# Attention scores as stacked rounded products, and the tile output taken from its bank by ScalarE

## The chip, the cores and the metric

The kernel runs on one core of one Trainium2 chip. Its time is the device time of one launch in microseconds (us); the median of three runs before the change is 2268.42 us (2266.53 to 2269.19).

## What is computed

One step of a one-layer backbone over 1152 tokens: 128 context tokens and 1024 latent tokens, width 1024. A first SwiGLU feed-forward part, an input projection, an attention group beside a recurrent group, an output projection, a second feed-forward part, a final norm. The change is in the attention group, four heads of two score maps each:

```python
q, k = rope(q), rope(k)                      # latent tokens only
k_all = concat(k, cached_k)                  # 1024 + 128 keys of 64 numbers, for each of m = 0, 1
s = einsum('bqhmd,bkhmd->bhmqk', q, k_all) * 64 ** -0.5
p = softmax(s)                               # in float32
pd = p[:, :, 0] - lam * p[:, :, 1]
o = pd @ v_all                               # 128 numbers per head
o = rmsnorm(o, subln_g) * (1 - lam_init)
```

Context tokens attend to the 128 context keys alone, latent tokens to 1152 keys.

## The kernel before

All tensors lie with features on the 128 partitions and tokens along the free dimension. Large products (feed-forward, projections) are made of two rounded parts of each factor (fp32r: high = the rounded value, low = the rest), as three products high·high, high·low and low·high of 128 x 384 columns (`three`, lines 715 to 719). Attention scores, in contrast, are plain f32 products.

Attention runs over 36 tiles `u` of 128 queries: nine a head, of which the first (`u % 9 == 0`) is the context tile with 128 keys and the other eight have 1152 keys. Each engine has its own list in a fixed order, and semaphores tie them. In a round `u` of the loop:

- TensorE (`scores(u)`, line 1043) makes both score maps. Map `m` has its 64 numbers on the partitions `64m` to `64m+63`, so a product uses half of the array's rows, and the six products of a tile (512, 512 and 128 keys for each map) alternate between the halves. Each f32 product leaves two records in the trace. Map 0 lies in banks 0 to 2, map 1 in banks 3 to 5. Map `m` of tile `u` may be written when the exponential of map `m` of tile `u-1` has been read (`e_done`). Then come the nine transposes of tile `u-2` in groups of three (`group`, line 1058, bank 6; a group waits until the copy of the one before it is done, `t_done`), with the value products of tile `u-3` between them (`values`, line 1072, bank 7; the first waits for `o_done` of the tile before it).
- VectorE takes both maxima (line 2286), copies the middle group of transposes (line 2310), forms the difference of the two maps of tile `u-1` (lines 2292 to 2295), and scales the output of tile `u-3` by the reciprocal sum out of bank 7 into SBUF (`output`, line 2303).
- ScalarE copies the first group of transposes (line 1557), takes both exponentials with their sums (line 1564), copies the third group, and squares the output of tile `u-4` from SBUF with its sum (line 1572).

`x` holds the queries (slots 0 to 3) and keys (slots 4 to 7) during attention. VectorE rotates the eight in place (`rope`), then multiplies the four recurrent outputs (line 2253), prepares lambda, and goes to the tiles; meanwhile TensorE makes the value projection in 18 parts, whose evacuations (line 1482) are ScalarE's. SyncE (SP) issues all DMAs of the kernel before; GpSimd (POOL) only scales outputs near the end of attention.

Of the kernel before, what the change touches and what calls it, by code (L numbers as in the profile page):

```python
# [62 lines left out]
PIECES = ((0, 0, 512), (0, 512, 1024), (1, 0, 512), (0, 1024, UNIT), (1, 512, 1024), (1, 1024, UNIT))  # L63
# [46 lines left out]
def build(nc, a, out):  # L110
    ctx = ExitStack()
    with ctx:
# [20 lines left out]
        lnorm = sb("lnorm", [P, 32])  # L133
        raw = sb("raw", [P, SLOTS, 1024])
        x = sb("x", [P, KT, T])
        tmp = sb("tmp", [P, 5, CH])
# [9 lines left out]
        with ExitStack() as s:  # L146
            hid_raw = sb("hid_raw", [P, NC * KT * CH], F32, s)
        hL = sb("hL", [P, NC * KT * CH], F32R, acts)
# [16 lines left out]
        mid = ExitStack()  # L165
        wiH = sb("wiH", [P, 2, 1024], F32R, mid)
# [15 lines left out]
        with ExitStack() as s:  # L182
# [10 lines left out]
            nlam = sb("nlam", [P, 1], F32, s)  # L193
        mid.close()
# [84 lines left out]
        roped = sem("roped")  # L279
        s_ready = sem("s_ready")  # L280
# [24 lines left out]
        psf = ps[:].rearrange("p b n -> p (b n)")  # L305
# [175 lines left out]
        def _(sp):  # L481
# [195 lines left out]
            load_raw(0, used_wo[0], a["w_out"][0])  # L677
            load_raw(1, used_wo[1], a["w_out"][1])

            sp.wait_ge(outs, 48)  # L680
            sp.wait_ge(spilled, 16 * KT)
            for hd in range(NH):
                sp.wait_ge(s_ready, (hd + 1) * 2 * QT)
                for k in (hd, hd + NH):
                    sp.dma_start(x[:, k], xd[k]).then_inc(xback, 16)
# [15 lines left out]
        def _(pool):  # L701

            pool.wait_ge(o_rec, 1)
# [9 lines left out]
        def _(pe):  # L713
# [319 lines left out]

            def scores(u):

                hd, q = u // QT, u % QT
                for m, b, e in ((0, 0, P), (1, 0, P)) if q == 0 else PIECES:
                    if b == 0 and 2 * u + m > 1:
                        pe.wait_ge(e_done, 2 * u + m - 1)
                    r = slice(m * DH, (m + 1) * DH)  # L1040
                    at = CTX if q else 0
                    keys = kc[r, hd] if b == LAT else x[r, hd + NH, at + b:at + e]
                    mm = pe.matmul(unit(u, m)[:, b:e], x[r, hd, q * P:(q + 1) * P], keys, start=True, stop=True,  # L1043
                                   tile_position=(m * DH, 0))
                    if e == (UNIT if q else P):
                        mm.then_inc(s_ready, 1)
# [1451 lines left out]
```

## Time and profile before

| | |
|---|---|
| median of three runs | 2268.42 us |
| span of the profiled execution, first to last instruction (the profile gives no other time of it) | 2266.8 us |
| TensorE (PE) busy | 2191.9 us, 97% |
| VectorE (DVE) busy | 1552.2 us, 68% |
| ScalarE (ACT) busy | 815.4 us, 36% |
| attention, first scores to last value products | about 1130 to 1352 us of the span |

How to read it: busy shares are means over stages that are bound by different things. TensorE's records overlap, so its busy time says that it had work in hand, not that it ran at its peak. The stage of the change is a tenth of the span, and its own rows are what counts.

### The profile page before, as it was taken

The page shows a single profiled execution, that of the slowest core. Times are in us where ns is not written, and L with a number is a line of the kernel's source. Part 1 is how long each engine was busy: PE and PEld are TensorE (multiplying, and loading weights), DVE is VectorE, ACT ScalarE, POOL GpSimd, SP SyncE. Part 2 cuts the span into 40 slices and gives each one's busy share as a digit, 9 for nine tenths or more (in the row PEclk, how much of TensorE's full clock was granted, in tenths as well). Part 3 has the DMA queues.
Part 4 walks back from the last instruction along what each step waited for, and adds up shares of the span by engine and source line. Part 5 has one row for each costly group of instructions (what it writes and reads, how often), then busy time and mean ns, then how long its engine had stood idle before and what let it go on. Part 6 is the DMA issues. An engine that isn't in the chain of part 4 may idle for free.

```text
span 2266.8 us, 33980 instructions
## 1 busy us (share of the span) xinstructions
PE 2191.9 (97%) x13144; PEld 2105.5 (93%) x13144; DVE 1552.2 (68%) x2607; ACT 815.4 (36%) x1458; POOL 20.1 (1%) x31
## 2 busy tenths in 40 slices
PE   5999999999999999999999999999999999999997
PEld 4989999999999999889977779899999999999996
DVE  6977777778888776666668874686454556756556
ACT  5532222334111144654255662353232323421122
POOL 0000000000000000000000030000000000000000
PEclk9999999999999999999999999999999999999998
DMA  7433333344624304010110011132212123431312
GB/s 290 133 105 135 103 126 111 113 138 131 213 78 158 126 27 151 19 47 28 32 49 22 22 40 38 56 114 68 78 59 86 58 87 101 159 120 52 109 41 84
DMA packets 82292, 210.10 MB, mean 93 GB/s; under 512 B 9856, under 2 KB 36352, under 8 KB 82176
## 3 DMA queue, kind: packets, MB, share of 16 engines
q1 hardware_dynamic: 82176, 208.52, 27.4%
q8 instruction: 78, 1.28, 0.2%
q14 instruction: 38, 0.31, 0.0%
HBM read 172.56 MB, written 35.92 MB: 92 GB/s over the span
## 4 chain that ended last, share of the span: by engine, by line
PE 88%; DVE 7%; ACT 2%; DMA 1%; issue 1%; SPq 0%; DVEq 0%; ACTq 0%
PE ps L717 15%; PE ps L719 15%; PE ps L718 15%; PE ps L792 9%; PE ps L793 9%; PE ps L794 9%; PE ps L972 6%; PE ps L1043 4%; PE ps L1072 2%; PE ps L1058 1%; PE ps L954 1%; DVE sb_nmx L2286 1%; DVE sb_hL L1752 1%; DVE sb_tmp L1761 1%; PE ps L741 1%
## 5 line engine op out<-in xcount | busy, mean ns | idle before, releaser
L717 PE MATMUL ps<-sb_hH,sb_wH 128*128 128x384 f32 x1664 | 562.7, 338 | 10.2 <-DVE sb_hL L1752 4.7
L719 PE MATMUL ps<-sb_hH,sb_wL 128*128 128x384 f32 x1664 | 557.4, 335 | 0.0
L718 PE MATMUL ps<-sb_hL,sb_wH 128*128 128x384 f32 x1664 | 557.3, 335 | 0.0
L717 PEld LDWEIGHTS ps<-sb_hH,sb_wH 128*128 128x128 f32 x1664 | 313.4, 188 | 17.5 <-DVE sb_hL L1752 6.0
L718 PEld LDWEIGHTS ps<-sb_hL,sb_wH 128*128 128x128 f32 x1664 | 313.4, 188 | 1.1
L719 PEld LDWEIGHTS ps<-sb_hH,sb_wL 128*128 128x128 f32 x1664 | 313.4, 188 | 0.0
L2062 DVE SCALAR_TENSOR_TENSOR sb_x<-ps,sb_mod,sb_x 128x384 f32<-128x384 f32 (+2 forms) x384 | 186.2, 513 | 172.6 <-PE ps L719 167.2
L792 PE MATMUL ps<-sb_hH,sb_wH 128*128 128x384 f32 x704 | 236.1, 335 | 4.1 <-DVE sb_tmp L1922 3.9
L793 PE MATMUL ps<-sb_hL,sb_wH 128*128 128x384 f32 x704 | 235.9, 335 | 0.0
L794 PE MATMUL ps<-sb_hH,sb_wL 128*128 128x384 f32 x704 | 235.8, 335 | 0.0
L1226 ACT ACTIVATE sb_wH<-sb_wide 128x512 fp32r<-128x512 f32 x176 | 110.8, 633 | 229.1 <-DVE sb_wide L1806 224.0
L1215 ACT ACTIVATE sb_wH<-sb_raw 128x512 fp32r<-128x512 f32 x212 | 129.7, 627 | 172.3 <-PE ps L719 69.2
L1360 ACT ACTIVATE sb_wH<-sb_raw 128x512 fp32r<-128x512 f32 (+1 forms) x96 | 56.8, 596 | 371.0 <-PE ps L719 363.4
L1788 DVE TENSOR_TENSOR sb_wL<-sb_raw,sb_wH 128x512 fp32r<-128x512 f32 x212 | 139.7, 685 | 58.5 <-ACT sb_wH L1215 58.1
L794 PE MATMUL ps<-sb_r2H,sb_wL 128*128 128x384 f32 x528 | 176.4, 334 | 0.0
L792 PE MATMUL ps<-sb_r2H,sb_wH 128*128 128x384 f32 x528 | 176.4, 334 | 0.0
L793 PE MATMUL ps<-sb_r2L,sb_wH 128*128 128x384 f32 x528 | 176.4, 334 | 0.0
L792 PEld LDWEIGHTS ps<-sb_hH,sb_wH 128*128 128x128 f32 x704 | 132.7, 188 | 5.2 <-issue 5.2
L794 PEld LDWEIGHTS ps<-sb_hH,sb_wL 128*128 128x128 f32 x704 | 132.8, 189 | 0.0
L793 PEld LDWEIGHTS ps<-sb_hL,sb_wH 128*128 128x128 f32 x704 | 132.6, 188 | 0.0
L1812 DVE TENSOR_TENSOR sb_wL<-sb_wide,sb_wH 128x512 fp32r<-128x512 f32 x176 | 114.0, 684 | 2.4 <-DVE sb_rq L1863 1.1
L2286 DVE TENSOR_REDUCE sb_nmx<-ps 128x1 f32<-128x1152 f32 (+1 forms) x72 | 85.8, 1233 | 39.3 <-PE ps L1043 39.3
(244 smaller groups left out, 3789.3 us busy)
## 6 DMA issues: line engine op xcount, KB each, us to landing
sb_raw<-in_w_gate SPq DMA_DIRECT2D x56, 512.0 KB, 3.7
sb_raw<-in_w_up SPq DMA_DIRECT2D x56, 512.0 KB, 3.6
sb_raw<-in_w_mod SPq DMA_DIRECT2D x56, 512.0 KB, 3.5
hidden<-sb_tmp SPq DMA_DIRECT2D x132, 192.0 KB, 2.2
sb_hid_raw<-hidden SPq DMA_DIRECT2D x40, 576.0 KB, 6.5
sb_raw<-in_w_dn SPq DMA_DIRECT2D x80, 256.0 KB, 2.7
sb_stage<-in_w_mod SPq DMA_DIRECT2D x4, 2048.0 KB, 15.4
sb_raw<-in_w_in SPq DMA_DIRECT2D x16, 512.0 KB, 3.5
```

The lines of the kernel that those rows point to most:

```text
L717: pe.matmul(o, wH, xH, start=begin, stop=False)
L718: pe.matmul(o, wH, xL, start=False, stop=False)
L719: return pe.matmul(o, wL, xH, start=False, stop=end)
L792: pe.matmul(dst, wH[:, slot, at], opv(0, b, k), start=begin and k == 0, stop=False, skip_group_check=True)
L793: pe.matmul(dst, wH[:, slot, at], opv(1, b, k), start=False, stop=False, skip_group_check=True)
L794: m = pe.matmul(dst, wL[:, slot, at], opv(0, b, k), start=False, stop=k == 3, skip_group_check=True)
L972: m = pe.matmul(dst, (wiH, wiH, wiL)[part][:, f, at], hv((hH, hL, hH)[part], c, k), start=s == 0, stop=s == 3 * KT - 1)
L1215: act.activation(wH[:, o if slot is None else slot], raw_of(o, other), ACT.Copy).then_inc(one_hi[o], 1)
L1226: act.activation(wH[:, at], wide[:, 8 + at], ACT.Copy).then_inc(sum_hi, 1)
L1788: dve.tensor_tensor(wL[:, at], raw_of(o, other), wH[:, at].bitcast(F32), ALU.subtract).then_inc(one_lo[o], 1)
L1812: dve.tensor_tensor(wL[:, at], wide[:, 8 + at], wH[:, at].bitcast(F32), ALU.subtract).then_inc(sum_lo, 1)
L2062: m = dve.scalar_tensor_tensor(x[:, t, b:e], ps[:, DOWN_BANKS[n % 6], b - c * CH:e - c * CH], mod[:, gate + t, cond:cond + 1], x[:, t, b:e ...
```

## The change

1. Score products of latent tiles are made of rounded parts. For each head and for queries and keys, ScalarE writes the high part of the 1024 columns into one buffer `qk_split` (`qk_high`) and VectorE the low part over `x` itself (`qk_low`). GpSimd then issues DMAs from SBUF to SBUF: the high queries of each map are put twice on the partitions (top and bottom half), and the keys of each map as high part on the map's own half and low part on the other half. So one product over all 128 rows gives high·high + high·low, and a second over 64 rows gives low query times high key. The cached keys `kc` get high and low parts once.
2. Each map of a tile takes three products of 384 keys over 128 rows and three of 384 keys over 64 rows; the latter alternate between the two maps. The map now lies in three banks with 384 columns each, and maxima and exponentials read and write through a view of three pieces.
3. The order of a tile's scores is: map 0 stacked (after `e_done` of map 0), then the low products of both maps (after `e_done` of map 1), then map 1 stacked. `s_ready` of map 0 comes with the last low product.
4. Head 0 is split before the tiles, among the value evacuations; heads 1 to 3 in the rounds 1, 3, 5, 7, 11, 13 on ScalarE and one round later on VectorE.
5. VectorE's `output` is gone. ScalarE squares the tile's output straight from bank 7 with the reciprocal sum as its scale, one round earlier than before, and then writes the scaled output itself.
6. The two first loads of `w_out` are issued after head 0, since their slots hold its queries until then.

```diff
+SPLIT_AT = {1: (1, 0), 3: (1, 1), 5: (2, 0), 7: (2, 1), 11: (3, 0), 13: (3, 1)}
         def unit(u, m):
-            return psf[:, m * 1536:m * 1536 + KEY_TILES[u % QT] * P]
+            return ps[:, 3 * m:3 * m + 3, 0:CH] if u % QT else ps[:, 3 * m, 0:P]
+        def tile_hi(hd, is_k):
+            return 2 * hd + is_k + 1 + (hd > 0)
...
+            def stack_queries(hd):
+                pool.wait_ge(qk_hi, tile_hi(hd, 0))
+                if hd == 0:
+                    for s in range(2):
+                        pool.wait_ge(raw_used[s], used_wo[s] + 1)
+                elif hd == 1:
+                    pool.wait_ge(v_ready, 18)
+                for m, r in ((0, top), (1, bottom)):
+                    for to in (top, bottom):
+                        pool.dma_start(queries(hd)[to, m], qk_split[r]).then_inc(qk_moved, 16)
+            def stack_keys(hd):
+                pool.wait_ge(qk_hi, tile_hi(hd, 1))
+                if hd:
+                    pool.wait_ge(qk_in, 96 * hd)
+                if hd == 3:
+                    pool.wait_ge(s_ready, 2 * QT)
+                for m, r in ((0, top), (1, bottom)):
+                    pool.dma_start(keys_of(hd)[r, m, 0:LAT], qk_split[r]).then_inc(qk_moved, 16)
+                pool.wait_ge(qk_lo, tile_hi(hd, 1))
+                lows = qk_rest[:, hd + NH, CTX:T]
+                for m, r, to in ((0, top, bottom), (1, bottom, top)):
+                    pool.dma_start(keys_of(hd)[to, m, 0:LAT], lows[r]).then_inc(qk_in, 16)
+                pool.wait_ge(qk_lo, 3)
+                for m, r, to in ((0, top, bottom), (1, bottom, top)):
+                    pool.dma_start(keys_of(hd)[r, m, LAT:UNIT], kcH[r, hd]).then_inc(qk_in, 16)
+                    pool.dma_start(keys_of(hd)[to, m, LAT:UNIT], kcL[r, hd]).then_inc(qk_in, 16)
+            for hd in range(NH):
+                stack_queries(hd)
+                stack_keys(hd)
...
+            def scores(u):
+                hd, q = u // QT, u % QT
+                if q == 0:
+                    context_scores(u)
+                    return
+                if q == 1:
+                    pe.wait_ge(qk_lo, tile_hi(hd, 0))
+                    pe.wait_ge(qk_moved, 96 * hd + 96)
+                    pe.wait_ge(qk_in, 96 * hd + 96)
+                pe.wait_ge(e_done, 2 * u - 1)
+                stacked_scores(u, 0, True)
+                pe.wait_ge(e_done, 2 * u)
+                for p in range(3):
+                    mm = low_scores(u, 0, p, False)
+                    low_scores(u, 1, p, True)
+                mm.then_inc(s_ready, 1)
+                stacked_scores(u, 1, False).then_inc(s_ready, 1)
...
+            def qk_high(hd, is_k):
+                if hd or is_k:
+                    act.wait_ge(qk_moved, 96 * hd + 64 * is_k)
+                    act.wait_ge(qk_lo, tile_hi(hd, is_k) - 1)
+                act.activation(qk_split[:], x[:, hd + NH * is_k, CTX:T], ACT.Copy).then_inc(qk_hi, 1)
             for n in range(15):
+                if n == 4:
+                    qk_high(0, 0)
+                elif n == 10:
+                    qk_high(0, 1)
+                    act.wait_ge(acst, N_ACST)
+                    act.activation(kcH[:], kc[:], ACT.Copy).then_inc(qk_hi, 1)
...
             def out_squares(u):
-                act.wait_ge(o_done, u + 1)
+                act.wait_ge(o_ready, u + 1)
                 act.wait_ge(o_ss, u + 1)
-                act.activation(tmp[:, 3, 0:P], attended(hd, t), ACT.Square,
+                act.activation(tmp[:, 3, 0:P], ps[:, 7, 0:P], ACT.Square, scale=rec[:, u % 6, 0:1],
                                accum_out=ss[:, hd, t:t + 1]).then_inc(o_ss, 1)
+                act.activation(attended(hd, t), ps[:, 7, 0:P], ACT.Copy, scale=rec[:, u % 6, 0:1]).then_inc(o_done, 1)
...
+                if u in SPLIT_AT:
+                    qk_high(*SPLIT_AT[u])
                 p_copy(u - 2, 2)
-                if u >= 4:
-                    out_squares(u - 4)
+                if 3 <= u < TILES + 3:
+                    out_squares(u - 3)
...
+            def qk_low(hd, is_k):
+                xt = x[:, hd + NH * is_k, CTX:T]
+                dve.wait_ge(qk_hi, tile_hi(hd, is_k))
+                dve.tensor_tensor(qk_rest[:, hd + NH * is_k, CTX:T], xt, qk_split[:].bitcast(F32),
+                                  ALU.subtract).then_inc(qk_lo, 1)
+            qk_low(0, 0)
+            qk_low(0, 1)
+            dve.wait_ge(qk_hi, 3)
+            dve.tensor_tensor(kcL[:], kc[:], kcH[:].bitcast(F32), ALU.subtract).then_inc(qk_lo, 1)
             dve.wait_ge(acst, N_ACST)
...
-                if u >= 3:
-                    output(u - 3)
+                if u - 1 in SPLIT_AT:
+                    qk_low(*SPLIT_AT[u - 1])
```

## Rows read from the trace of the kernel before

**Rows 1.** The page: engines' busy time, share of the span, instructions.
```profile
PE 2191.9 (97%) x13144; PEld 2105.5 (93%) x13144; DVE 1552.2 (68%) x2607; ACT 815.4 (36%) x1458; POOL 20.1 (1%) x31
```
**Rows 2.** Stretches: busy us (instructions) by engine, granted clock, DMA share, GB/s.
```profile
1183.60:1234.60 51.00, 49.20 (x321) 37.13 (x320) 42.06 (x63) 30.93 (x71) 0.00 (x0) 1.00 0.07 24
1149.20:1157.00 7.80, 7.08 (x20) 4.83 (x20) 4.56 (x5) 2.67 (x4) 0.00 (x0) 0.60 0.15 61
1360.00:1400.00 40.00, 38.09 (x228) 37.18 (x227) 18.55 (x38) 10.45 (x19) 0.00 (x0) 1.00 0.09 27
```
**Rows 3.** Timeline of one tile: start, duration, engine, line, instruction, count [idle before].
```profile
1171.90 2.62 DVE L2286 TENSOR_REDUCE sb_nmx<-ps 128x1 f32<-128x1152 f32 x2 [0.73 <-PE ps L1043]
1172.19 0.55 PE L1058 MATMUL ps<-sb_ident,sb_pr 128*128 128x128 f32 x3
1172.78 0.49 ACT L1557 ACTIVATE sb_pT<-ps 128x384 f32<-128x384 f32 x1 [2.10 <-PE ps L1058]
1173.29 1.22 ACT L1564 ACTIVATE sb_pr<-ps,sb_nmx 128x1152 f32<-128x1152 f32 x1
...
1174.43 0.55 DVE L2310 COPY sb_pT<-ps 128x384 f32<-128x384 f32 x1
1174.55 1.22 ACT L1564 ACTIVATE sb_pr<-ps,sb_nmx 128x1152 f32<-128x1152 f32 x1
...
1175.04 0.55 PE L1058 MATMUL ps<-sb_ident,sb_pr 128*128 128x128 f32 x3
...
1175.34 1.42 DVE L2295 SCALAR_TENSOR_TENSOR sb_pr<-sb_pr,sb_coef 128x1152 f32<-128x1152 f32 x1
```
**Rows 4.** Timeline, the next tile's scores and the maxima after them.
```profile
1175.52 2.38 PE L1043 MATMUL ps<-sb_x 64*128 64x512 f32 x8
...
1177.76 2.62 DVE L2286 TENSOR_REDUCE sb_nmx<-ps 128x1 f32<-128x1152 f32 x2 [0.73 <-PE ps L1043]
```
**Rows 5.** Groups of instructions, 1153 to 1338 us: busy us, mean ns, idle before.
```profile
L2303 DVE TENSOR_SCALAR sb_v<-ps,sb_rec 128x128 f32<-128x128 f32 x23 | 7.9, 345 | 0.0
L1572 ACT ACTIVATE sb_tmp<-sb_v 128x128 f32<-128x128 f32 x22 | 6.8, 311 | 0.0
```
**Rows 6.** The chain of waits over a head's first tiles: start, us, what.
```profile
1183.61 2.62 DVE sb_nmx L2286 x2
...
1189.08 1.16 PE ps L1072 x10
...
1193.96 2.62 DVE sb_nmx L2286 x2
...
1199.82 1.37 DVE sb_nmx L2286
...
1201.21 1.32 ACT sb_pr L1564 x2
```
**Rows 7.** Timeline of the stretch before the tiles, VectorE, ScalarE, TensorE.
```profile
1114.30 3.89 DVE L2253 TENSOR_TENSOR sb_xr<-sb_xr,sb_xg 128x1152 f32<-128x1152 f32 x3
1123.71 0.22 DVE L2274 TENSOR_TENSOR sb_dl<-sb_dl 128x64 f32<-128x64 f32 x1 [5.53 <-DMA sb_dl<-in_dl]
1113.15 1.22 DVE L1670 TENSOR_TENSOR sb_wiL<-sb_raw,sb_wiH 128x1024 fp32r<-128x1024 f32 x1 [3.37 <-ACT sb_wiH L1164]
1104.10 0.94 ACT L1482 ACTIVATE sb_v<-ps 128x256 f32<-128x256 f32 x3 [9.21 <-DVEq L2265]
1112.07 1.05 ACT L1164 ACTIVATE sb_wiH<-sb_raw 128x1024 fp32r<-128x1024 f32 x1
1131.35 3.94 PE L1043 MATMUL ps<-sb_x 64*128 64x512 f32 x8 [0.91 <-ACT sb_pr L1564]
1149.24 4.19 PE L1043 MATMUL ps<-sb_x 64*128 64x512 f32 x7 [2.43 <-ACT sb_pr L1564]
```
**Rows 8.** DMA issues from 1040 to 1160 us: KB each, median us to landing.
```profile
sb_kc<-in_kc SPq DMA_DIRECT2D x1, 256.0 KB, 3.5
out_v<-sb_v SPq DMA_DIRECT2D x1, 256.0 KB, 2.1
```

More of the change, by code:

```diff
@@ L133, in build @@
         lnorm = sb("lnorm", [P, 32])
+        with ExitStack() as s:
+            q_first = sb("q_first", [P, 2, LAT], F32R, s)
         raw = sb("raw", [P, SLOTS, 1024])
+        with ExitStack() as s:
+            qk_rest = sb("qk_rest", [P, KT, T], F32R, s)
         x = sb("x", [P, KT, T])
+        with ExitStack() as s:
+            qk_split = sb("qk_split", [P, LAT], F32R, s)
         tmp = sb("tmp", [P, 5, CH])
@@ L147, in build @@
             hid_raw = sb("hid_raw", [P, NC * KT * CH], F32, s)
+        with ExitStack() as s:
+            qstack = sb("qstack", [P, NH - 1, 2, LAT], F32R, s)
+            kstack1 = sb("kstack1", [P, 2, UNIT], F32R, s)
         hL = sb("hL", [P, NC * KT * CH], F32R, acts)
@@ L165, in build @@
         mid = ExitStack()
+        with ExitStack() as s:
+            kstack2 = sb("kstack2", [P, 2, UNIT], F32R, s)
         wiH = sb("wiH", [P, 2, 1024], F32R, mid)
@@ L279, in build @@
         roped = sem("roped")
+        qk_hi = sem("qk_hi")
+        qk_lo = sem("qk_lo")
+        qk_moved = sem("qk_moved")
+        qk_in = sem("qk_in")
         s_ready = sem("s_ready")
@@ L303, in build, with by_bank, queries, keys_of @@
         ssf = ss[:].rearrange("p h t -> p (h t)")
-        psf = ps[:].rearrange("p b n -> p (b n)")
         o_first = raw[:, 2:4].rearrange("p a n -> p (a n)")
         def unit(u, m):
-            return psf[:, m * 1536:m * 1536 + KEY_TILES[u % QT] * P]
+            return ps[:, 3 * m:3 * m + 3, 0:CH] if u % QT else ps[:, 3 * m, 0:P]
+        def by_bank(row):
+            return row.rearrange("p (a n) -> p a n", a=3)
+        def queries(hd):
+            return qstack[:, hd - 1] if hd else q_first[:]
+        def keys_of(hd):
+            return (kstack0, kstack1, kstack2, kstack0)[hd]
+        def tile_hi(hd, is_k):
+            return 2 * hd + is_k + 1 + (hd > 0)
         def probs(u, m):
@@ L683, in _ @@
                 sp.wait_ge(s_ready, (hd + 1) * 2 * QT)
+                if hd == 0:
+                    load_raw(0, used_wo[0], a["w_out"][0])
+                    load_raw(1, used_wo[1], a["w_out"][1])
                 for k in (hd, hd + NH):
@@ L1032, in outputs, with context_scores, stacked_scores @@
                 m.then_inc(ot_ready, 1)
+            def context_scores(u):
+                hd = u // QT
+                for m in range(2):
+                    if u:
+                        pe.wait_ge(e_done, 2 * u + m - 1)
+                    r = slice(m * DH, (m + 1) * DH)
+                    pe.matmul(unit(u, m), x[r, hd, 0:P], x[r, hd + NH, 0:P], start=True, stop=True,
+                              tile_position=(m * DH, 0)).then_inc(s_ready, 1)
+            def stacked_scores(u, m, begin):
+                hd, q = u // QT, u % QT
+                for p in range(3):
+                    mm = pe.matmul(ps[:, 3 * m + p, 0:CH], queries(hd)[:, m, (q - 1) * P:q * P],
+                                   keys_of(hd)[:, m, p * CH:(p + 1) * CH], start=begin, stop=not begin)
+                return mm
@@ L1034, in scores, with low_scores @@
+            def low_scores(u, m, p, begin):
+                hd, q = u // QT, u % QT
+                r = slice(m * DH, (m + 1) * DH)
+                return pe.matmul(ps[:, 3 * m + p, 0:CH], qk_rest[r, hd, q * P:(q + 1) * P],
+                                 keys_of(hd)[r, m, p * CH:(p + 1) * CH], start=begin, stop=not begin,
+                                 tile_position=(m * DH, 0))
             def scores(u):
                 hd, q = u // QT, u % QT
[L1037 to L1046, printed above, removed]
+                if q == 0:
[8 more added lines that the diff above has]
+                pe.wait_ge(e_done, 2 * u)
+                for p in range(3):
+                    mm = low_scores(u, 0, p, False)
+                    low_scores(u, 1, p, True)
+                mm.then_inc(s_ready, 1)
+                stacked_scores(u, 1, False).then_inc(s_ready, 1)
```

23 lines of the change are left out of this document (11 added, 12 removed).

## Prediction

> **What bounds the kernel now.** Busy times of the page first [rows 1]: TensorE has 97%. But its share is a mean, so I read the busy table by stretches for the stage of the change. Over one head (51.0 us, nine tiles) TensorE has 49.2 us of records, VectorE 42.1, ScalarE 30.9, at full clock throughout [rows 2]. So if TensorE's work shrinks, VectorE is next, 18% below.
>
> Then the timeline of a tile in steady state [rows 3, 4]; the chain of waits and the DMA issues serve for heads' edges and the start. Let 0 be the start of its first maximum, 1171.90. VectorE: both maxima until 2.53, copy of the middle transposes 2.53 to 3.1, difference until 4.86 (1175.34 + 1.42), then `output` 0.35 [rows 5], then it idles 0.73. TensorE: first transposes at 0.29, value products, second transposes, and then the third transposes at 3.14 (1175.04), right after VectorE's copy (1174.43 + 0.55 = 1174.98). The next scores start at 3.62 (1175.52) and free VectorE at 5.86 (1177.76). So the chain of a tile is maxima, copy, third transposes, scores: 5.86 us, of which 2.24 are scores until map 0 is ready and 2.7 lie between the third transposes and that point. TensorE and VectorE alternate in it; a shorter score part shortens it until VectorE's own 4.86 us bound it.
>
> **Scores, part by part.** What a product costs: fp32r products of 384 columns over 128 rows run at 228 in 38.09 us [rows 2], 0.167 each, their weight loads hidden. f32 value products leave ten records of 128 columns in 1.16 us [rows 6], 0.11 each, so a record of 512 columns would take about 0.43, and a tile's scores (eight of 512, four of 128) 3.9 us one after another. They take 2.24 until map 0 is ready (1175.52 to 1177.76 [rows 4]) and 0.29 more until the first transposes (1171.90 to 1172.19 [rows 3]), 2.5. So the two halves of the array do run side by side, though not quite from start to end.
>
> New tile: 3 stacked (0.50), 3 pairs of low ones side by side (0.50), 3 stacked (0.50), and two changes between whole and half array, 0.1 each (the third transposes' three records would be issued in 0.33, but the scores start 0.48 after them, 1175.04 to 1175.52): 1.7 instead of 2.5.
>
> Chain over VectorE and TensorE: third transposes at 3.14, their three records 0.33, stacked of map 0 until 4.0, change 0.1, low products issued 4.1 to 4.6, the last one ends about 0.33 after its issue (its record's length): map 0 ready at about 4.85. Chain over ScalarE, which is new because map 0 is ready only after the exponential of map 1: after map 0's readiness the stacked products of map 1 (0.36 left to issue) stand where the tail of the old scores stood (0.29), so the first copy stays at 0.9, the exponentials at 1.39 and 2.65 [rows 3]; with the sum's read, TensorE is released 1.36 after the second one's start, at 4.0; low products 0.73: 4.75. VectorE alone: 4.86 plus hand-over 0.03. Three limits within 0.15 of each other; I take 4.88, a saving of 0.98 a tile.
>
> The Trainium skill speaks of the change between whole and split array: "TensorEngine Tiling (Array Packing)", Tiling Modes, says that changing the mode drains TensorE. The trace agrees, with about 0.1 us a change, and a tile has two of them before and after, so nothing in the sum moves.
>
> Steps of a head that differ: the two over the context tile, 1183.61 to 1193.96, 10.35 long, lose `output` in the first, 0.3, where VectorE alone is the chain, and 1.0 in the second, where it is TensorE from transposes to scores; the one to 1199.82: 0.98; the next, about 5.2, waits for the exponentials at 1201.21 [rows 6]: the low products now wait for the second of them, released at 1203.85, ready 1204.6: 0.4; two steps of 6.0 and three of 5.86: 5 x about 1.0. Sum 7.75 a head, 23.2 for heads 1 to 3. Head 0 from its third tile: five steps of 1.0: 5.0. Its first three: the scores at 1131.35 take 4.1 at a clock that starts at half speed [rows 7], about 2.9 after: 1.2; the second tile 0.9; the third starts at 1149.24 after 2.43 idle, at half clock (mean 0.60 until 1157) [rows 2] and takes 4.24: now it waits 1.3 longer for the second exponential and needs 1.3 after it: 1.65 saved. 3.8 in all. **Saved by scores: 32.0.**
>
> **The output from its bank.** VectorE loses 0.35 a tile, already in its 4.86. ScalarE gains a copy of 128x128, as the square: 0.31 [rows 5]. Its list a tile: copy, two exponentials, copy, square and sum read end at 4.8, now 5.1. `o_done` then comes at 5.15 instead of 4.8 or so; the value products that wait for it start at 4.88 + 0.7 = 5.6, and ScalarE's next copy at 5.8. Hidden by 0.4; gone, it would cost as much as it is late. At the end of attention square and copy replace scale and square: nothing (between -0.3 and +0.5).
>
> **Maxima and exponentials over three banks.** Same element counts (3 x 384 = 1152), other view. No row has it; from 0 to 0.1 each (a tenth of the step between the 384-column copy's 0.55 and a maximum's 1.3). I take 0.03 on two maxima: 2.0 over 32 tiles, with what the three close limits add.
>
> **Splits in the rounds.** Six on each engine: ScalarE 1.05, VectorE 1.22 (the cast and the low part of 1024 columns of a weight tile) [rows 7]. ScalarE's stands after both exponentials, ahead of the third copy and the output. Behind it: `o_done` at 6.2, so the value products of the next round start 0.7 late, the second transposes end 0.5 after VectorE is ready to copy them, and its list ends at 4.86 + 0.5; then comes its own split, 1.22. Sum 1.7, since VectorE has no slack left. In round 1 both fall into waits: ahead of the tile that starts at 1149.24 TensorE idles 2.43, behind it a tile's scores take 4.2 [rows 7] and VectorE has nothing else. 5 x 1.7 = 8.5; between 1.2 each, 6, if the first part is absorbed, and 2.3 each, 11.4, if nothing overlaps.
>
> **The start of head 0.** GpSimd's twelve moves are in no row. The engines' steps: `qk_high(0,0)` after the value evacuation at 1104.10, until 1105.6; those behind it wait 1.05 more, which TensorE, six banks ahead, does not see. Queries move from there. VectorE reaches `qk_low(0,0)` after the recurrent products, 1118.2 (1114.30 + 3.89), ends 1119.4; ScalarE `qk_high(0,1)` until 1120.5; VectorE's low keys 1121.8. The cached keys' part waits for the last constant, 1123.7 [rows 7]: ScalarE 0.6, VectorE 0.7: 1125.0. Then four small moves. Value evacuations 10 and 11 wait behind that on ScalarE until 1124.7; TensorE needs their banks only after 1129, and lambda's steps move 1.3 later with 3.4 in hand. TensorE asks at 1131.3. So the moves have 6.3 us after 1125.0 and 10.8 after 1120.5. By SP's moves of 256 KB, landed 2.1 to 3.5 after issue [rows 8], all is there by 1129 when issues overlap; if each of the last four is 2.5 and they are served one by one, 1135: 3.7 late. I take 1 us, range 0 to 8.
>
> By the Trainium skill, "DMA: Bandwidth & Descriptors", Anatomy of one DMA, a GpSimd-issued DMA takes about 2.0 us plus its bytes over 436 GB/s; that is an estimate of 2.6 for 256 KB; with overlap it makes the start free, and the time 1 less, 2247.4. No run here shows it yet.
>
> The two loads of `w_out` come 40 us later but still 100 before their cast: nothing. The context tile's f32 products stay.
>
> **Sum.** 32.0 - 2.0 - 8.5 - 1.0 - 0.5 (small delays at the tail of attention, where nothing else changes and later loads follow attention's own marks) = 20.0. Against the span: 2266.8 - 20.0 = 2246.8. The median of the runs is 1.6 above that span, and I put the same around the new one: **2248.4**. Own range 2242 (splits 6, no view cost, start free: 25.5 and a little) to 2254.
>
> **Rivals.** (a) The low fp32r pairs don't overlap (weight loads for each of six short products, 64 rows): +0.5 in every chain, period 5.35. For it: no fp32r product over 64 rows in the trace. Against: the f32 ones overlap, so do their loads. 32.0 - 15.5, view cost vanishes in slack, splits 6, start 1: 9.5 saved, 2258.9.
>
> (b) Moves late by 8 at the start, or the clock: TensorE idles 1.7 at five splits, and after 2.43 idle it ran at half speed [rows 2, 7]. Half a tile's work at half clock costs 2: 5 x 2 = 10 more. Against: over heads 1 to 2 gaps of this kernel left the clock at 1.00. Either one: 2257.
>
> (c) VectorE's maxima over three pieces cost 0.2 more each: 0.4 x 32 = 12.8: 2259.
>
> (d) Slower: moves issued by GpSimd are served one at a time and take p each. Behind `qk_high(0,1)` wait four query moves (cover 13.9), behind the scores four key moves and four small ones, say 6p against 10.8. Loss (4p - 13.9) + (6p - 10.8) eats the gain of 20 at p = 4.5. At p = 5 it is 25, ScalarE's splits in rounds 3 and 5 then wait about 4 each for `qk_moved` in front of copies: 2248.4 + 24 (1 was counted) + 8 = 2280. For it: GpSimd issues no DMA before, each here changes partitions and writes fp32r; against: SP's 256 KB land in 3.5 at worst [rows 8].
>
> The Trainium skill, "SBUF — State Buffer", in its warning on the DVE blocks DMA trap, speaks for (d): it says that GpSimd cannot write descriptors while VectorE runs an operation in a two-port mode. VectorE's operations here are mostly two-input or read a bank, for which it does not claim this; no run here shows it.
>
> **Chances.** Forecast 0.60, (a) 0.10, (b) 0.12, (c) 0.06, (d) 0.08, a mix of them without net effect 0.04. No change means within 0.2%, 4.5 us, what a measurement of this kernel can tell. Faster 0.87, same 0.04, slower 0.09. Range 2238 to 2262: all of the forecast and nearly all of (a) to (c); the low end is VectorE's work as the bound of each head (42.1 - 3.1, 39 us, or 12 saved a head on three, less splits).
>
> **What would show it.** Maxima 4.9 apart in steady tiles (5.35: a); 12 score records a tile spaced 0.17, low pairs within 0.05 of each other; the third transposes still right after VectorE's copy; five steps of 6.6 after rounds 3, 5, 7, 11 and 13; the second scores at 1131.4 (later: b, d); clock 1.00 over heads 1 to 3; VectorE over 90% busy. I am wrong if the steady step is over 5.3, or the start is late by more than the splits cost.

## The result and the profile after

The changed kernel takes 2247.59 us (median of 4 runs, 2246.44 to 2250.51) against 2268.63 for the kernel before in the same session: ratio 0.9912, 95% interval 0.9898 to 0.9926, 21 us less by the medians and 20 by the ratio. A second measurement of the same file gave 2247.28 (0.9903, 0.9888 to 0.9919). The forecast was 2248.4. The profiled spans are 2246.1 and 2266.8, 20.7 apart.

The page's busy times and three stretches of the trace answer to [rows 1, 2] (us, then busy us and instructions of PE, PEld, DVE, ACT, POOL, granted clock, DMA share, GB/s):

```profile
PE 2166.9 (96%) x13144; PEld 2103.6 (94%) x13144; DVE 1552.5 (69%) x2580; ACT 834.0 (37%) x1503; POOL 47.2 (2%) x79
```
```profile
1183.60:1234.60 51.00, 46.62 (x354) 40.19 (x353) 45.83 (x63) 38.12 (x94) 9.13 (x18) 1.00 0.45 121
1149.20:1157.00 7.80, 6.23 (x31) 4.56 (x31) 7.08 (x9) 4.49 (x9) 0.00 (x0) 0.78 0.45 93
1230.57:1274.67 44.10, 41.85 (x319) 36.49 (x319) 39.52 (x55) 33.07 (x81) 0.00 (x0) 1.00 0.08 29
```

The third stretch is head 2, from its first maximum to head 3's: 44.10 us, where the kernel before had 50.97. VectorE has 90% of it (before 82%), TensorE still 95%.

To say where the 20.7 went I cut the attention stage at the starts of the maxima. It begins with the first row and ends with the last; the middle row is the last tile's maxima. First the kernel before, then after:

```profile
1130.51 0.49 DVE L2286 TENSOR_REDUCE sb_nmx<-ps 128x1 f32<-128x128 f32 x2 [0.60 <-PE ps L1043]
...
1337.56 2.62 DVE L2286 TENSOR_REDUCE sb_nmx<-ps 128x1 f32<-128x1152 f32 x2 [0.64 <-PE ps L1043]
...
1365.96 0.67 DVE L2349 TENSOR_SCALAR sb_v<-sb_v,sb_ss 128x128 f32<-128x128 f32 x3
```
```profile
1131.27 0.49 DVE L2415 TENSOR_REDUCE sb_nmx<-ps 128x1 f32<-128x128 f32 x2 [0.60 <-PE ps L1110]
...
1315.78 2.62 DVE L2415 TENSOR_REDUCE sb_nmx<-ps 128x1 f32<-128x1152 f32 x2
...
1345.24 0.67 DVE L2471 TENSOR_SCALAR sb_v<-sb_v,sb_ss 128x128 f32<-128x128 f32 x3
```

The stage went from 235.45 to 213.97, 21.5 less. Its start moved 0.76 later; over the profiles of all runs it lies between 1130.0 and 1132.8, and the latest is that of a kernel without any edit ahead of the stage (E2 below), so I don't count this as an effect of the change. The part behind the stage is equal (900.8). The steps between first maxima, worked out from VectorE's timeline between those rows, tile by tile (`|` parts the heads; each list of a head ends with the step to the next head's context tile):

```
before 4.77 11.20 7.00 6.56 6.00 5.86 5.86 5.85 5.05 | 5.30 5.86 5.19 6.00 6.00 5.86 5.86 5.85 5.05 |
       5.29 5.86 5.20 6.00 6.00 5.86 5.86 5.86 5.04 | 5.30 5.86 5.19 6.00 6.00 6.42 6.33 5.86, end 28.40
after  3.22 11.31 5.45 5.61 6.31 4.96 6.19 4.96 6.19 | 3.49 4.96 4.86 5.91 4.97 6.18 4.97 4.98 4.78 |
       4.64 4.97 4.86 4.96 4.98 4.98 4.96 4.96 4.79 | 4.63 4.98 4.85 4.99 4.97 6.71 5.02 4.96, end 29.46
```

By head, saved and (in brackets) what the prediction's terms give for it: head 0 3.95 (8.8 - 0.5 - 5.1 - 1.0 = 2.2), head 1 5.87 (7.75 - 0.5 - 3.4 = 3.85), head 2 6.87 (7.25), head 3 with the end 4.79 (6.75).

**The steady tile** (timeline of after, answers to [rows 3, 4]):

```profile
1254.98 2.62 DVE L2415 TENSOR_REDUCE sb_nmx<-ps 128x1 f32<-128x1152 f32 x2
...
1255.51 0.49 PE L1158 MATMUL ps<-sb_ident,sb_pr 128*128 128x128 f32 x3
...
1256.04 0.49 ACT L1670 ACTIVATE sb_pT<-ps 128x384 f32<-128x384 f32 x1 [1.07 <-PE ps L1158]
...
1257.52 0.55 DVE L2432 COPY sb_pT<-ps 128x384 f32<-128x384 f32 x1
...
1258.17 0.50 PE L1158 MATMUL ps<-sb_ident,sb_pr 128*128 128x128 f32 x3
...
1258.43 0.77 PE L1117 MATMUL ps<-sb_kstack,sb_qstack 128*128 128x384 f32 x3
1258.43 1.42 DVE L2425 SCALAR_TENSOR_TENSOR sb_pr<-sb_pr,sb_coef 128x1152 f32<-128x1152 f32 x1
1258.76 0.20 ACT L1677 ACTIVATION_READ_ACCUMULATOR sb_pr<-ps,sb_nmx 128x1 f32 x1
...
1259.13 0.80 PE L1125 MATMUL ps<-sb_kstack,sb_qk_rest 64*128 64x384 f32 x6
...
1259.86 0.79 PE L1117 MATMUL ps<-sb_kstack,sb_qstack 128*128 128x384 f32 x3
1259.96 2.62 DVE L2415 TENSOR_REDUCE sb_nmx<-ps 128x1 f32<-128x1152 f32 x2
```

The maxima over three banks still take 2.62. The third transposes start 3.19 after the first maximum, 0.1 behind VectorE's copy and without a gap behind TensorE's own value products. The single records' starts of TensorE, from 1258.43 on, are 0.26, 0.17, then 0.264 to the first low pair, 0.279, 0.177 between pairs (the two of a pair 0.003 apart), and 0.265 to the stacked products of map 1, 0.278, 0.174. So low pairs do run side by side, and a change of the array costs about 0.1 at the change and 0.1 more at the product behind it: 0.2, where I had 0.1. Over the whole tile no spacing is longer than 0.29: TensorE issues without a pause from tile to tile, and its own list makes the step 4.97. Of that, 2.92 go to transposes and value products (1255.51 to 1258.43) and 2.05 to scores. The low products also wait for ScalarE's second exponential, but that wait isn't what ended last: the change ahead of them (0.264 and 0.279) takes no more than the change back (0.265 and 0.278), which waits for nothing.

**A step with a split**, with VectorE's low part (L2394) in it:

```profile
1159.78 0.56 DVE L2432 COPY sb_pT<-ps 128x384 f32<-128x384 f32 x1 [0.29 <-PE ps L1158]
...
1160.69 1.42 DVE L2425 SCALAR_TENSOR_TENSOR sb_pr<-sb_pr,sb_coef 128x1152 f32<-128x1152 f32 x1
1162.03 1.22 DVE L2394 TENSOR_TENSOR sb_qk_rest<-sb_x,sb_qk_split 128x1024 fp32r<-128x1024 f32 x1
1163.17 2.62 DVE L2415 TENSOR_REDUCE sb_nmx<-ps 128x1 f32<-128x1152 f32 x2
```

Here 6.19 = 4.77 (VectorE's list without gaps, measured in E8) + 0.29 idle, which goes when ScalarE's high part is made small (E4), so is that part's, arriving by way of the transposes, + 1.14 (1.22 less the overlap). Over the steady 4.97 that is 1.22.

**The start.** GpSimd's moves and the second scores (timeline), and the moves' landing (DMA issues, 1100 to 1340: KB each, median us from issue to landing); the last row answers to [rows 7], 1131.35:

```profile
1121.52 1.02 POOL L759 DMA_DIRECT2D sb_kstack<-sb_qk_split  x2 [12.79 <-ACT sb_qk_split L1645]
1122.78 1.02 POOL L763 DMA_DIRECT2D sb_kstack<-sb_qk_rest  x2 [0.24 <-DVE sb_qk_rest L2394]
...
1127.61 0.53 POOL L767 DMA_DIRECT2D sb_kstack<-sb_kcL  x1
```
```profile
sb_qstack<-sb_qk_split POOLq DMA_DIRECT2D x12, 256.0 KB, 4.3
sb_kstack<-sb_kcL POOLq DMA_DIRECT2D x8, 32.0 KB, 2.9
```
```profile
1132.19 1.01 PE L1117 MATMUL ps<-sb_kstack,sb_q_first 128*128 128x384 f32 x3 [1.00 <-ACT sb_pr L1677]
```

Each issue takes 0.51, those of a group overlap, and the last landed at about 1129.4 (the four small ones of this head took 1.8 to 2.3 us each, less than the median of all). The scores waited for ScalarE's exponential (its end at 1132.2), not for a move, as before the change: the start cost nothing.

### The profile page after: what moved, and what is told of

The parts are those of the page before. It is cut to its first block, busy times and chain, and to the rows that moved or that the text cites. A ratio compares the mean times of both kernels' runs of the same rounds, so it can differ in the third digit from the quotient of the medians.

```text
span 2246.1 us, 34066 instructions
## 1 busy us (share of the span) xinstructions
PE 2166.9 (96%) x13144; PEld 2103.6 (94%) x13144; DVE 1552.5 (69%) x2580; ACT 834.0 (37%) x1503; POOL 47.2 (2%) x79
## 3 DMA queue, kind: packets, MB, share of 16 engines
q8 instruction: 78, 1.28, 0.2%
## 4 chain that ended last, share of the span: by engine, by line
PE 89%; DVE 7%; ACT 2%; issue 1%; DMA 1%; SPq 0%; DVEq 0%; ACTq 0%
PE ps L786 16%; PE ps L788 16%; PE ps L787 16%; PE ps L861 9%; PE ps L862 9%; PE ps L863 9%; PE ps L1041 7%; PE ps L1172 2%; DVE sb_nmx L2415 1%; PE ps L1023 1%; PE ps L1117 1%; DMA sb_stage<-in_w_mod 1%; PE ps L1158 1%; PE ps L1125 1%; ACT sb_pr L1677 1%
## 5 line engine op out<-in xcount | busy, mean ns | idle before, releaser
L2002 DVE TENSOR_TENSOR sb_tmp<-ps,sb_tmp 128x384 f32<-128x384 f32 x32 | 17.9, 558 | 120.2 <-PE ps L863 119.1
```

## The experiments

Each kernel of the table ran beside the kernel before on one chip: E1, E2, E3 and E5 on one, the changed kernel again, E4, E6 and E7 on a second, E8 to E10 on a third. The kernel before had medians of 2268.26, 2268.20 and 2268.35 there. Medians, ratio with 95% interval, and the attention stage cut as above:

| | us | ratio | stage |
|---|---|---|---|
| changed kernel again | 2247.28 | 0.9903 (0.9888-0.9919) | 213.8 |
| E1 output on VectorE | 2247.50 | 0.9905 (0.9887-0.9923) | 213.7 |
| E2 output part alone | 2271.64 | 1.0015 (1.0005-1.0025) | 236.3 |
| E3 low parts on GpSimd | 2247.21 | 0.9900 (0.9883-0.9917) | 214.0 |
| E4 high parts small | 2246.85 | 0.9906 (0.9889-0.9923) | 213.3 |
| E5 low products not paired | 2249.67 | 0.9916 (0.9896-0.9936) | 214.3 |
| E6 splits at context tiles | 2253.61 | 0.9935 (0.9922-0.9949) | 220.0 |
| E7 moves one by one | 2289.96 | 1.0091 (1.0073-1.0109) | 256.6 |
| E8 low products left out | 2245.13 | 0.9894 (0.9877-0.9910) | 211.8 |
| E9 low products on one half | 2264.73 | 0.9982 (0.9972-0.9992) | 230.8 |
| E10 last keys at a context tile | 2247.50 | 0.9904 (0.9888-0.9921) | 214.7 |

**The same again.** 

> The changed kernel as it is, beside the following ones on their chip, as their measure: 2247.6, every theory.

It repeats to 0.3 us in the median and 0.2 in the stage.

**E1, the output back on VectorE**, and the square back to a read from SBUF, one round later; the rest of the change kept.

```diff
-                act.activation(tmp[:, 3, 0:P], ps[:, 7, 0:P], ACT.Square, scale=rec[:, u % 6, 0:1],
+                act.activation(tmp[:, 3, 0:P], attended(hd, t), ACT.Square,
...
-                act.activation(attended(hd, t), ps[:, 7, 0:P], ACT.Copy, scale=rec[:, u % 6, 0:1]).then_inc(o_done, 1)
...
+            def output(u):
...
+                dve.tensor_scalar(attended(u // QT, u % QT), ps[:, 7, 0:P], rec[:, u % 6, 0:1], None, ALU.mult).then_inc(o_done, 1)
```

> The changed kernel with the output's scaling given back to VectorE and the square back to a read from SBUF, one round later. Theory (VectorE, the chain over TensorE and the chain over ScalarE all near 4.9 us a tile): VectorE's 4.87 becomes 5.22, the steady step 5.25 instead of 4.97, over about 27 such steps +7.6, with the context steps +8: about 2255.5. Rival (the chain over TensorE and ScalarE bounds, VectorE has room): within 1 us of 2247.6, steps stay 4.97.

No difference in time. VectorE's rows in a steady tile:

```profile
1254.17 2.61 DVE L2412 TENSOR_REDUCE sb_nmx<-ps 128x1 f32<-128x1152 f32 x2
...
1258.95 0.35 DVE L2430 TENSOR_SCALAR sb_v<-ps,sb_rec 128x128 f32<-128x128 f32 x1
1259.21 2.61 DVE L2412 TENSOR_REDUCE sb_nmx<-ps 128x1 f32<-128x1152 f32 x2
```

The step is 5.04: VectorE's 4.77 and 0.27 for the output. Since TensorE's own step is 4.97, the move of the output saves only 0.07 a tile, and the end of the stage (last maxima to last norm) is 28.51 here against 29.46 in the changed kernel: 0.95 of it is given back. My expected +8 took 4.87 for VectorE's list and added 0.35; they are 4.77 and 0.27, and the sum of 5.04 stands against TensorE's 4.97.

**E2, that part alone on the kernel before.**

> The kernel before with the output part alone: ScalarE squares and scales out of the bank, VectorE's output is gone, scores as before. Theory (a tile's chain is maxima, copy, third transposes, scores, and output stands in VectorE's idle time): steps stay 5.86, only the steps into the context tiles lose 0.3, about -1: 2267.6. Rival (VectorE's 0.35 times 36 counts): -12: 2256.

Steady steps stay at 5.86, the step into a context tile is 4.79 instead of 5.05 and the one behind it 5.52 instead of 5.30, and the end takes 29.34 instead of 28.40. So alone it costs 0.9 in the stage, where I expected 1 less: the gain into the context tile is given back behind it, and the end of the stage was not in my account. The measured difference of the medians is 3.4; in the profile another 2.3 lie ahead of the stage, which starts at 1132.82, and no edit stands there. What moved it is open.

**E5, the low products of map 1 first, then those of map 0**, to take the pairs apart.

```diff
-                    mm = low_scores(u, 0, p, False)
-                    low_scores(u, 1, p, True)
+                    low_scores(u, 1, p, True)
+                for p in range(3):
+                    mm = low_scores(u, 0, p, False)
```

> The changed kernel with the six low products in the order map 1 three times, then map 0 three times, instead of alternating. Theory (alternating products run side by side in the two halves of the array): map 0 is ready 0.5 us later, and with no room on that chain the steady step goes from 4.97 to about 5.45, over some 27 steps +13: 2260.5. Rival (they don't overlap, or the chain has room): the step stays 4.97, 2247.6.

Step 5.00 instead of 4.97: neither the 5.45 of the theory nor a proof of the rival. The records still start two by two, 0.009 apart, and six take as long as before. The trace doesn't say which map a record belongs to; but since products of one half start at least 0.17 apart (E9), I take two that start 0.009 apart to be one of each half, although the kernel lists three of one half before three of the other. So this did not make rival (a)'s case; E9 does.

**E9, both maps' low products on the upper rows** (map 1's low part is then another number).

```diff
-                r = slice(m * DH, (m + 1) * DH)
+                r = slice(0, DH)
...
-                                 tile_position=(m * DH, 0))
+                                 tile_position=(0, 0))
```

> The changed kernel with map 1's low products taken from map 0's rows (map 1's scores then carry a wrong low part), so both maps' low products use the upper 64 rows and can't run side by side. The same count, the same columns, the same changes of the array. It is the case of the prediction's rival (a), which the earlier run with another order of issue did not make. Theory: six records 0.167 apart instead of three pairs: 0.5 more a tile, steady step 4.97 + 0.5 = 5.47, 24 to 28 tiles: 11 to 14 us longer than the changed kernel. If each short product also waits for its weights (rows hold the same number, 128 columns), more: 0.06 each, 0.36 a tile, another 10 us. If the step stays at 4.97, side-by-side running is not what gives the saving.

Step 5.48, 0.51 more, for three records of 0.17 more: side-by-side running is shown to be worth that. VectorE's and TensorE's rows in a steady step:

```profile
1261.28 2.62 DVE L2415 TENSOR_REDUCE sb_nmx<-ps 128x1 f32<-128x1152 f32 x2 [0.47 <-PE ps L1125]
...
1263.95 0.56 DVE L2432 COPY sb_pT<-ps 128x384 f32<-128x384 f32 x1
...
1264.64 0.49 PE L1158 MATMUL ps<-sb_ident,sb_pr 128*128 128x128 f32 x3
...
1265.59 1.31 PE L1125 MATMUL ps<-sb_kstack,sb_qk_rest 64*128 64x384 f32 x6
...
1266.76 2.62 DVE L2415 TENSOR_REDUCE sb_nmx<-ps 128x1 f32<-128x1152 f32 x2 [0.47 <-PE ps L1125]
```

The six low records take 1.31 instead of 0.80. TensorE still issues without a pause over the whole step (no spacing above 0.29) and VectorE waits 0.47 for scores: 0.51 put on TensorE's list came out whole in the step, which is what a step set by that list does. Only in the tile whose value products are the context tile's (two records instead of eighteen) does TensorE wait for VectorE's copy, 0.83, and there the step is 5.34.

The whole time is 17 us longer, where I expected 11 to 14. Of the stage's 16.8, 6.9 lie in head 0's first five steps (38.81 us for 31.90), with a granted clock of 0.74 there instead of 0.89, so part of the 6.9 is the clock; whether the longer products made it lower is open. The other 9.9 are the longer steps.

**E8, low products left out**: one of three a map kept in head 1, none in head 2.

> The changed kernel with low products left out: in head 1 one of three a map is left, in head 2 none (their scores are then less exact); heads 0 and 3 are as in the changed kernel. It asks what the steady step of 4.97 us is made of. Theory: TensorE is full in it (records without a gap) with 0.2 us for each of the two changes between whole and half array, and VectorE's own list, 4.87, is next. Then head 1's steady steps (4.97 now) fall to 4.87 to 4.90 and not by the 0.33 us of the four products, with TensorE idle 0.2 a tile; head 2's are the same 4.87 to 4.90, with TensorE idle about 0.9. From the last stacked record of map 0 to the first of map 1, now 0.26 + 0.3 + 0.3 + 0.17 or so, head 2 leaves one spacing of 0.17. Rival: the chain over ScalarE (map 0 is only ready after the exponential of map 1) sets 4.97; then head 2, where map 0 still carries the wait for that exponential, stays near 4.97 less the part of the low products that lay behind it, and VectorE idles. Whole time: 14 tiles by 0.1 and the edges, 1 to 3 us less.

Both heads step at 4.77, without a gap on VectorE, while TensorE waits for it:

```profile
1252.12 2.62 DVE L2421 TENSOR_REDUCE sb_nmx<-ps 128x1 f32<-128x1152 f32 x2
...
1255.25 0.31 PEld L1164 LDWEIGHTS ps<-sb_ident,sb_pr 128*128 128x128 f32 x3 [0.30 <-DVE sb_pT L2438]
...
1255.56 1.42 DVE L2431 SCALAR_TENSOR_TENSOR sb_pr<-sb_pr,sb_coef 128x1152 f32<-128x1152 f32 x1
1256.89 2.61 DVE L2421 TENSOR_REDUCE sb_nmx<-ps 128x1 f32<-128x1152 f32 x2
```

Two pairs out should give 0.35, and the step falls by 0.20 to the next limit. So 4.97 is TensorE's list and VectorE's is 4.77 (I expected 4.87 to 4.90).

The rival, the chain over ScalarE, is not settled by this run as I meant it to be. In head 2 map 0 doesn't keep the wait for the exponential: its `s_ready` comes with the last stacked product, which is issued ahead of that wait. In head 1 it keeps it, but with two pairs fewer behind it, so 4.77 there only says that this chain is at most 4.77 + 0.35 = 5.12 in the changed kernel. What rules it out is the steady tile of the changed kernel, where the change that waits takes no longer than the one that doesn't. The room is small: ScalarE's read ends at 1258.96 and the low products start at 1259.13, and where TensorE did stand waiting for such a read (E9, 1254.71 to 1254.77) it took 0.06. That leaves about 0.1, an estimate of 4.86 for this chain.

In head 2, where the array is never changed, the records of the six stacked products start 0.26, 0.18, 0.18, 0.24 and 0.17 apart: 0.08 of the 0.2 that I put down to the first change is there without a change too, at the product that waits for the exponential and the one behind it.

The Trainium skill, "TensorEngine Tiling (Array Packing)", Tiling Modes, says that a change of mode drains TensorE and gives no time for it. The trace agrees in that a change costs: 0.2 us where nothing is waited for (0.265 and 0.278 instead of 0.17 each), some 0.4 of a tile of 4.97.

**E4, ScalarE's high parts of heads 1 to 3 over 16 columns instead of 1024.**

> The changed kernel with the high parts of heads 1 to 3 reduced from 1024 to 16 columns on ScalarE (the rest of the buffer keeps head 0's keys, so these heads' scores are not the reference's); VectorE's low parts stay whole. Theory by the changed kernel's trace (steps after ScalarE's part stay 4.96, so it is hidden): no change, 2247.6, within 1. Rival (the prediction's first part of a split, 0.5 a piece on VectorE's and TensorE's waits): -2.5, 2245.

The median doesn't tell it from the changed kernel, but three steps of 6.19 become 5.91 (4.77 + 1.14): the 0.29 ahead of VectorE's copy is what ScalarE's part costs. The other steps don't move, apart from head 0's first five, where this profile has another clock (1.00 from 1131 to 1136 and 0.50 from 1149 to 1157).

**E3, the low parts of heads 1 to 3 on GpSimd.**

```diff
+                pool.tensor_tensor(qk_rest[:, hd + NH * is_k, CTX:T], xt, qk_split[:].bitcast(F32),
+                                   ALU.subtract).then_inc(qk_lo, 1)
...
-                if u - 1 in SPLIT_AT:
-                    qk_low(*SPLIT_AT[u - 1])
```

> The changed kernel with the low parts of heads 1 to 3 made by GpSimd between its moves instead of by VectorE. In the changed kernel's trace a step with such a part on VectorE is 6.19 instead of 4.97, but the one before the context tile is given back (3.49 after it instead of 4.64). Theory: four steps shrink by 1.22, -5: 2242.7, with GpSimd's own time (unknown, 3 to 10 us each) hidden. Rival (prediction's 1.7 each, with ScalarE's share): -8.5, 2239. Rival (GpSimd's and VectorE's two-input operations block each other): VectorE's differences or maxima get longer where a part runs, gain below 2, or a loss.

No gain, where I expected 5: 2247.21. VectorE's list is freed of 1.22, but one of its smallest instructions is held up until GpSimd's ends:

```profile
1148.08 2.40 POOL L743 TENSOR_TENSOR sb_qk_rest<-sb_x,sb_qk_split 128x1024 fp32r<-128x1024 f32 x1
...
1148.31 2.19 DVE L2434 SCALAR_TENSOR_TENSOR sb_coef<-sb_sums,sb_nlam,sb_rec 128x1 f32<-128x1 f32 x1
```

Its end, 1150.50, is that of GpSimd's, 1150.48. Beside two more of the six parts it takes 1.24 and 1.64, beside the others at most 0.27; in the changed kernel it takes 0.22 in these rounds. A maximum, which reads a bank, keeps its 1.35 beside a part. Both instructions of the rows read two operands from SBUF. The Trainium skill, "SBUF — State Buffer", Who interferes with whom, says that a VectorE instruction with two SBUF inputs contends with a GpSimd instruction that reads SBUF, and that the one which comes second is blocked; the trace agrees, with 2.19 instead of 0.22.

Step by step, rounds 4 to 17 took 1.4 less than in the changed kernel and the first four steps 1.6 more (27.15 us for 25.59). Their granted clock was 0.77 instead of 0.87, so how much of the 1.6 is the hold-up of 2.19 and how much the clock is open.

**E6, splits of heads 2 and 3 put next to the context tiles.**

```diff
-SPLIT_AT = {1: (1, 0), 3: (1, 1), 5: (2, 0), 7: (2, 1), 11: (3, 0), 13: (3, 1)}
+SPLIT_AT = {1: (1, 0), 3: (1, 1), 7: (2, 0), 9: (2, 1), 16: (3, 0), 18: (3, 1)}
```

> The changed kernel with the splits in rounds 1, 3, 7, 9, 16, 18 instead of 1, 3, 5, 7, 11, 13, so that VectorE's low parts of heads 2 and 3 stand in the rounds about the context tiles, where it idles 1.17 and 0.45 or is given back 1.15. Theory: the visible ones are then only those of round 3 and part of 9 and 18: -3.3, 2244.3. Rival (a part costs its 1.22 wherever it stands): 2247.6.

Slower by 6 than the changed kernel, where I expected 3 less. The freed rounds do step at 4.97 and a low part ahead of a context tile is given back (6.18, then 3.49), but the second step behind each of these context tiles takes 11.12 and 9.54. ScalarE, GpSimd and SP there:

```profile
1188.96 1.06 ACT L1645 ACTIVATE sb_qk_split<-sb_x 128x1024 fp32r<-128x1024 f32 x1 [4.54 <-DMA sb_qstack<-sb_qk_split]
```
```profile
1177.36 2.04 POOL L749 DMA_DIRECT2D sb_qstack<-sb_qk_split  x4 [11.72 <-ACT sb_qk_split L1645]
```
```profile
1177.96 1.16 SPq L519 DMA_DIRECT2D sb_raw<-in_w_out  x2
1179.16 1.25 SPq L719 DMA_DIRECT2D sb_x<-x_spilled  x2
```

The four queries' moves were in flight with SP's loads at the end of the head (2.2 MB). The last landed 10.1 us after its own issue, 11.6 after the first, where the moves of head 3's queries in the changed kernel, with nothing beside them, took 4.2 in the median and 5.0 at most. The next high part writes the same buffer and waits for them in front of the exponentials. TensorE waited too, and its granted clock from 1188 to 1196 was 0.61, so part of the 11.12 is the clock.

**E10, only the last split moved** (13 to 16), whose moves nobody waits for.

> The changed kernel with the split of head 3's keys in round 16 instead of 13, so that VectorE's low part (round 17) stands ahead of a context tile, where the traces show that a late start of the list is given back (3.5 after it instead of 4.63). Theory: the step of 6.19 in head 1 goes to 4.97 and the one ahead of the context tile becomes 6.19 and then 3.50: 1.1 us less in head 1's rounds or 1.2 in the stage. SP's loads of two heads at the end of head 1 can meet the key moves (four of 256 KB), which was 11 us instead of 4.1 in another run, but nothing waits for these moves before round 28: no cost. Time 1.1 us less than the changed kernel, not to be told from it by the medians, only by the trace. Rival: the loads and moves delay something else and the gain is not seen.

Head 1's 6.18 in round 14 becomes 4.98, the step into the context tile 6.17 instead of 4.78, and the next 3.50 instead of 4.64: 1.0 less, as expected, and not visible in 2247.50. In head 0 this profile's steps were longer (7.07 for 5.61), at a granted clock of 0.59 instead of 0.79 from 1149 to 1157: that part varies from launch to launch.

**E7, GpSimd waits for each move before it issues the next.**

> The changed kernel with GpSimd waiting for each move to land before it issues the next. Landing is 4.1 us for 256 KB and 3.0 for 32 KB in the changed kernel's trace. Theory (overlap of the moves is what hides them; rival d of the prediction with p of 4): the keys of head 0 are complete about 1124 + 4 x 4.1 + 4 x 3.0 = 1152 instead of 1130.6, so the second scores start 20 us late, and rounds 3 and 5 wait for queries and keys of head 1, some 5 each: 2247.6 + 30, 2278. Rival (the moves have room enough in any order): under 2 us.

Slower than the kernel before by 0.9%, and than the changed kernel by 42, where I expected 30: rival (d)'s mechanism. TensorE at the second scores, and GpSimd's queue (one move of 256 KB, one of 32 KB):

```profile
1142.98 1.30 PE L1125 MATMUL ps<-sb_kstack,sb_q_first 128*128 128x384 f32 x3 [12.49 <-DMA sb_kstack<-sb_kcL]
```
```profile
1109.12 0.51 POOL L744 DMA_DIRECT2D sb_q_first<-sb_qk_split  x1 [2.64 <-DMA sb_q_first<-sb_qk_split]
...
1138.94 0.51 POOL L744 DMA_DIRECT2D sb_kstack<-sb_kcH  x1 [1.53 <-DMA sb_kstack<-sb_kcL]
```

A move occupies GpSimd for 3.1 (0.51 and 2.62 of waiting), a small one for 2.05. At the start 12 us more, then 5.1, 20.7 and 4.7 in rounds 4, 8 and 14: 43. In round 8 ScalarE waited 18.30 for the moves of head 2's queries, one of which kept GpSimd waiting 8.04 beside SP's loads, and TensorE behind that ran at a granted clock of 0.50 (1214 to 1220). The changed kernel doesn't pay this because its moves are in flight four at a time.

Issue to landing, from this run's DMA issues between 1100 and 1250:

```profile
sb_qstack<-sb_qk_split POOLq DMA_DIRECT2D x12, 256.0 KB, 2.9
sb_kstack<-sb_kcL POOLq DMA_DIRECT2D x6, 32.0 KB, 1.8
```

The Trainium skill, "DMA: Bandwidth & Descriptors", Anatomy of one DMA, gives the estimates 2.6 for 256 KB and 2.1 for 32 KB. For a move alone the trace has 2.9 and 1.8: near, with more for the bytes and less that is fixed. With others beside it, 256 KB took 4.0 to 4.3 in the median, and up to 10.1 beside SP's loads.

## Why the prediction was right

The time is right within 1 us. The mechanism is as forecast, a shorter chain that ends at the next limit of nearly 4.9; that the time is so near is luck, since errors of both signs, of up to 3.6 us, met. Against its own steps:

- **Steady step 4.88: measured 4.97.** The low pairs side by side, the order of the chain and the unchanged start of the third transposes are as forecast. The mis-sized term is TensorE: I worked out two chains and VectorE's list but not TensorE's own sum. By the prediction's terms it is 27 x 0.11 + 1.7 = 4.7, not above the others; measured, the 27 f32 records take 2.92 and the scores 2.05 instead of 1.7. A change, forecast at 0.1, is 0.2, and the record behind the first stacked one comes 0.26 after it instead of 0.17. So TensorE's list is the limit at 4.97 (E8, E9). VectorE's, which I had at 4.86, is 4.77: I read 1.42 to the end of its record, but the next instruction starts 0.09 before that. Three limits near 4.88 were really 4.97, 4.77 and, over ScalarE, about 4.86 by estimate, which no run isolates. The prediction's own terms for the chain over TensorE also give 4.77, not the 4.85 that it states (last low product issued at 4.43, plus 0.33). Some 24 steps by 0.09: 2 less saved.
- **Steps over the context tile, 1.3 a head: 0.9** (head 2: 5.04 to 4.79 and 5.29 to 4.64), some 1.2 less in three heads.
- **Maxima over three banks, 2.0: nothing**, 2.62 both.
- **Splits, 5 x 1.7 = 8.5: measured about 4.9.** Of the visible five, those in rounds 6, 12 and 14 cost 1.22, 0.95 and 1.2 over a step of 4.97 and the one in round 4 about 1.3. The one in round 8, ahead of the context tile, cost 1.4 (6.19 for 4.78) and gave 1.15 back in the step behind it (3.49 for 4.64). ScalarE's half, which I had at 0.5, is 0.29 (E4), and partly inside TensorE's lead over VectorE. That a late list is given back at a context tile was the step I had left out. The five steps, foretold as 6.6, are 6.31, 6.19, 6.19, 5.91 and 6.18.
- **Start, 1.0: nothing.** The second scores waited for ScalarE's exponential, not for a move.
- **Head 0**: its gain differs from profile to profile with the granted clock in its first tiles (0.78 over the stretch of [rows 2] where the kernel before had 0.60). At 1.00 from 1131 to 1136 the first two steps were 2.46 and 10.60 (E4, E6) instead of 3.22 and 11.31 at 0.66; the fourth was 5.61 at 0.79 from 1149 to 1157, and 7.07 to 7.09 at 0.50 to 0.59 (E4, E8, E10). The second step, which was to shrink by 0.9, did not. Over heads 1 and 2 the clock stayed at 1.00, as rival (b) would not have it.
- **Output from its bank: hidden**, but worth nothing: 0.07 a tile saved, and about 0.95 lost at the end (E1, E2), where I had 0.5 for all small delays there.
- **Head 3** saved 2 less than forecast: the end takes 29.46 instead of 28.40, and the steps of 6.71 and 5.02, where ScalarE loads its table twice (1.28 each, at 1299.09 and 1301.10), saved 1.0 instead of 2, from 6.42 + 6.33 to 11.73.

Together: 20.0 - 2.2 (steady) - 1.2 (context) + 2.0 (banks) + 3.6 (splits) + 1.0 (start) - 0.6 (end) - 1.0 (table loads) = 21.6, against 21.5 in the stage.

Rival (a) didn't happen, but its price was about right: E9 costs 9.9 outside head 0's first five steps, where (a) had 10.5, and 17 with them. Rival (c) is out. Rival (d) needed p = 4.5 if moves were served one by one; alone they are 3.1 and 2.05, and they overlap.

Not tested: no run has the rounded products in the old order, or f32 products in the new one, so what the new order alone (map 1's stacked products behind map 0's readiness) gives isn't told apart from what the rounded parts give.

## What to carry over

Where two engines alternate, write down each engine's own sum beside the chains: shortening a shared chain ends at the longest list, and here the lists were 4.97 and 4.77 with 0.07 left for an edit that looked like 0.35. Work put into such rounds costs little if it stands just ahead of a place with slack (a short tile), as long as its transfers don't meet others that land at the same place. Small edits that only free an engine are worth nothing until that engine is last, and can cost at the end of the stage.

## What the runs showed of the hardware

- Products of 64 rows on the two halves start 0.003 apart, and 0.009 apart when the kernel lists three of one half ahead of three of the other (E5); on one half they start 0.17 apart (E9).
- Changing between whole and half array: 0.1 at the change and 0.1 at the next product (0.265 and 0.278 instead of 0.17 each, in the steady tile).
- ScalarE's square of 128 x 128 took 0.37 from its bank with a scale, 0.31 from SBUF [rows 5]:

```profile
L1685 ACT ACTIVATE sb_tmp<-ps,sb_rec 128x128 f32<-128x128 f32 x36 | 13.2, 367 | 2.4 <-PE ps L1172 2.4
```
- A GpSimd subtraction over 1024 columns took 2.40, VectorE's 1.22, and stretched a VectorE instruction of 0.22 to 2.19 (E3).
